# The first block's rotary step: partner dimension read across partitions by VectorE instead of produced by a TensorE product

## The reference, cut to what matters

```
def apply_rope(t, cos, sin):
    tf = t.astype(jnp.float32).reshape(*t.shape[:-1], HEAD_DIM // 2, 2)
    c = cos[None, :, None, :]
    s = sin[None, :, None, :]
    t0, t1 = tf[..., 0], tf[..., 1]
    out = jnp.stack([t0 * c - t1 * s, t0 * s + t1 * c], axis=-1)
    return out.reshape(t.shape).astype(t.dtype)
...
        q = apply_rope(split_heads_norm(q, q_norm[layer], N_HEADS), cos, sin)
        k = apply_rope(split_heads_norm(k, k_norm[layer], N_KV_HEADS), cos, sin)
...
        attn = latent_attention(q, k, v, kc, vc)
```

## Time and profile before

| | |
|---|---|
| median of 3 runs | 2101.53 us |
| profiled execution, its span | 2097.6 us |
| busy: TensorE, weight loads, VectorE, ScalarE | 91%, 74%, 54%, 43% of the span |
| heads of layer 0 (about 51 to 125 us), of layer 1 (about 909 to 957 us) | 74 us, 48 us |
| instructions of the rotation product L923 | 40, two for each of 20 products |

### The profile page before, as it was taken

How to read it: one execution, slowest core, us unless ns; L and a number is a source line. 1 busy time by engine, 2 the same in 40 slices (tenths; PEclk the granted TensorE clock), 3 DMA queues, 4 the chain that set the end, 5 groups by cost and what they waited for, 6 DMA issues and landing times.

```text
span 2097.6 us, 33677 instructions
## 1 busy us (share of the span) xinstructions
PE 1903.2 (91%) x14126; PEld 1550.1 (74%) x14126; DVE 1133.1 (54%) x1862; ACT 892.0 (43%) x1516; POOL 16.9 (1%) x31
## 2 busy tenths in 40 slices
PE   7999989999999999999899999999999667777666
PEld 4877677778777888899699999997898444455444
DVE  3454766676787789557655667789665111110012
ACT  4333444565766667445444555644845000000001
POOL 0000000000000000000000000000000000000000
PEclk9999999999999999999999999999999998998888
DMA  8222014453555555224045555543247999999995
GB/s 313 88 71 80 1 72 143 162 202 104 170 172 180 191 193 177 89 93 161 1 167 196 171 188 185 183 161 121 81 151 304 419 421 419 419 419 420 421 420 233
DMA packets 91121, 428.00 MB, mean 204 GB/s; under 512 B 11089, under 2 KB 12754, under 8 KB 66002
## 3 DMA queue, kind: packets, MB, share of 16 engines
q1 hardware_dynamic: 78866, 382.51, 48.3%
q10 hardware_dynamic: 12096, 43.26, 6.1%
HBM read 424.68 MB, written 1.05 MB: 203 GB/s over the span
## 4 chain that ended last, share of the span: by engine, by line
PE 66%; DMA 19%; DVE 7%; ACT 3%; SPq 2%; issue 2%; DVEq 0%; POOL 0%; ACTq 0%; POOLq 0%
PE bank L463 43%; PE bank L1608 8%; DMA area<-in_w 7%; DMA ring<-in_w 4%; DMA his<-in_w 4%; DMA PPT<-in_w 2%; PE bank L478 2%; PE bank L2453 2%; DMA HH<-in_w 1%; DVE st L1270 1%; PE bank L1198 1%; SPq L2890 1%; PE bank L2497 1%; PE bank L2104 1%; ACT PPT L1215 1%
## 5 line engine op out<-in xcount | busy, mean ns | idle before, releaser
L463 PE MATMUL bank<-HH_r,his_r 128*128 128x256 f32 (+1 forms) x1504 | 505.0, 336 | 3.8 <-DVE ring_r L442 3.7
L463 PE MATMUL bank<-HH_r,ring_r 128*128 128x256 f32 (+1 forms) x1504 | 490.7, 326 | 0.0
L442 DVE TENSOR_TENSOR ring_r<-ring,his_r 128x1024 fp32r<-128x1024 f32 x306 | 373.7, 1223 | 216.2 <-ACT his_r L434 214.9
L463 PE MATMUL bank<-H_r,his_r 128*128 128x256 f32 (+1 forms) x1440 | 471.0, 327 | 0.0
L434 ACT ACTIVATE his_r<-ring 128x1024 fp32r<-128x1024 f32 x306 | 322.5, 1056 | 317.7 <-PE bank L463 234.1
L463 PEld LDWEIGHTS bank<-HH_r,his_r 128*128 128x128 f32 x1504 | 283.7, 189 | 38.0 <-issue 13.4
L463 PEld LDWEIGHTS bank<-HH_r,ring_r 128*128 128x128 f32 x1504 | 283.2, 188 | 27.1
L463 PEld LDWEIGHTS bank<-H_r,his_r 128*128 128x128 f32 x1440 | 270.9, 188 | 28.5 <-issue 2.6
L2469 DVE TENSOR_TENSOR tmp<-tmp,bank 128x128 f32<-128x128 f32 x64 | 18.4, 288 | 386.7 <-ACT tmp L2462 268.4
L2453 PE MATMUL bank<-area,KF 128*32 128x128 f32 x1888 | 88.3, 315 | 41.2 <-DMA area<-in_w 36.7
L463 PE MATMUL bank<-area_r,his_r 128*128 128x256 f32 (+1 forms) x384 | 122.1, 318 | 0.0
(11 more groups left out here) (412 smaller groups left out, 3318.4 us busy)
## 6 DMA issues: line engine op xcount, KB each, us to landing
area<-in_w SPq DMA_DIRECT2D x91, 1024.0 KB, 27.3
ring<-in_w_in SPq DMA_DIRECT2D x102, 512.0 KB, 3.5
ring<-in_w_gate_up SPq DMA_DIRECT2D x88, 512.0 KB, 3.5
ring<-in_w SPq DMA_DIRECT2D x36, 1024.0 KB, 27.1
HH<-in_w SPq DMA_DIRECT2D x26, 1024.0 KB, 26.8
ring<-in_w_down SPq DMA_DIRECT2D x44, 512.0 KB, 3.5
KX<-in_w_mod_rows ACTq DMA_DIRECT2D x28, 512.0 KB, 3.4
VX<-in_w_mod_rows ACTq DMA_DIRECT2D x28, 512.0 KB, 3.5
```

The source lines that it names most:

```text
L442: ve.eng.tensor_tensor(lo_slot(u), stream.slot(u), hi_slot(n).bitcast(F32), ALU.subtract).then_inc(*ve_lo.up(n))
L463: ins = pe.eng.matmul(out, a, b, start=k == 0 and m == 0, stop=end)
```

## The change: what it does

The order of the 128 dimensions of each query and key head of the first block becomes: the 64 even ones, then the 64 odd ones. This is done on the host, in the columns of w_in and in the two norm gains (`halves`). The cosine and sine tables follow that order, the sine negated for the second half. A dimension's partner then lies 64 partitions away. The rotation product and its matrix go; VectorE multiplies, in two operations on 64 partitions each, one half of the head by the sine table of that half and writes the result to the other half of tmp[2]. It then waits for both before it overwrites the head with the cosine product. The constants become two columns narrower.

```diff
-CON = {"ident": 0, "sel": 128, "rope": 130, "cos": 258, "sin": 514, "dftc": 770, ...}
+CON = {"ident": 0, "sel": 128, "cos": 256, "sin": 512, "dftc": 768, ...}
-NCON = 2818
+NCON = 2816
...
-        def pe_rope_step(pe, l, i):
-            out = banks.take((ve_rope, ("sin", l, i)), "rope", l, i)
-            pe.wait_ge(*banks.emptied("rope", l, i))
-            pe.wait_ge(*landed["dft"])
-            pe.wait_ge(*ac_out.at("head", l, i))
-            pe.eng.matmul(out[:, 0:256], cc("rope"), heads(l)[i][3][:, 0:256], start=True, stop=True).then_inc(*pe_rope.up(l, i))
...
             pe_head_sums(pe, l, 0)
-            pe_rope_step(pe, l, 0)
             pe_values_projected(pe, l)
             pe_head_sums(pe, l, 1)
-            pe_rope_step(pe, l, 1)
...
                 if i > 2:
                     pe_head_sums(pe, l, i - 1)
-                    pe_rope_step(pe, l, i - 1)
...
             pe_head_sums(pe, l, 9)
-            pe_rope_step(pe, l, 9)
...
         def ve_rope_step(ve, l, i):
             x = heads(l)[i][3][:, 0:256]
             ve.wait_ge(*ve_rope.last())
-            ve.wait_ge(*pe_rope.at(l, i))
-            ve.eng.tensor_tensor(tmp[2][:, 0:256], banks.ap("rope", l, i)[:, 0:256], cc("sin", 0, 256),
-                                 ALU.mult).then_inc(*ve_rope.up("sin", l, i))
+            ve.wait_ge(*landed["dft"])
+            ve.wait_ge(*ac_out.at("head", l, i))
+            for to, of in ((slice(0, 64), slice(64, P)), (slice(64, P), slice(0, 64))):
+                ve.eng.tensor_tensor(tmp[2][to, 0:256], x[of, :], cc("sin", 0, 256)[of, :],
+                                     ALU.mult).then_inc(*ve_rope.up("sin", l, i, to.start))
+            ve.wait_ge(*ve_rope.last())
             ve.eng.tensor_tensor(x, x, cc("cos", 0, 256), ALU.mult).then_inc(*ve_rope.up("cos", l, i))
             ve.wait_ge(*ve_rope.last())
             ve.eng.tensor_tensor(x, x, tmp[2][:, 0:256], ALU.add).then_inc(*ve_rope.up("roped", l, i))
...
+def halves(w):
+
+    a = w.reshape(w.shape[:-1] + (-1, 64, 2))
+    return np.swapaxes(a, -1, -2).reshape(w.shape)
...
-        put(("q_norm", l), cols(I["q_norm"][l]))
-        put(("k_norm", l), cols(I["k_norm"][l]))
+        put(("q_norm", l), cols(halves(I["q_norm"][l])))
+        put(("k_norm", l), cols(halves(I["k_norm"][l])))
...
-        "w_in": tiles(I["w_in"], paired(W_IN_ORDER, 8, (10,))),
+        "w_in": tiles(np.concatenate([halves(I["w_in"][:, :, 0:1280]), I["w_in"][:, :, 1280:]], axis=2), paired(W_IN_ORDER, 8, (10,))),
```

More of the change, by code:

```diff
@@ L72 @@
 NVEC = _vec_layout()
-CON = {"ident": 0, "sel": 128, "rope": 130, "cos": 258, "sin": 514, "dftc": 770, "dfts": 1282, "idfc": 1794, "idfs": 2306}
+CON = {"ident": 0, "sel": 128, "cos": 256, "sin": 512, "dftc": 768, "dfts": 1280, "idfc": 1792, "idfs": 2304}
 NCON0 = 130
-NCON = 2818
+NCON = 2816
 FIL = {"z": 0, "decay": 256}
@@ L84, in shape_constants @@
     con[:, 0:128] = np.eye(P)
-    for i in range(64):
-        con[2 * i + 1, CON["rope"] + 2 * i] = -1.0
-        con[2 * i, CON["rope"] + 2 * i + 1] = 1.0
     late = np.zeros((P, 3, P), np.float32)
@@ L97, in shape_constants @@
     ang = np.concatenate([row[:, None] * inv, col[:, None] * inv], axis=1).astype(np.float32)
-    con[:, CON["cos"]:CON["sin"]] = np.repeat(np.cos(ang.astype(np.float64)), 2, axis=1).T
-    con[:, CON["sin"]:CON["dftc"]] = np.repeat(np.sin(ang.astype(np.float64)), 2, axis=1).T
+    con[:, CON["cos"]:CON["sin"]] = np.tile(np.cos(ang.astype(np.float64)).T, (2, 1))
+    con[:, CON["sin"]:CON["dftc"]] = np.concatenate([np.sin(ang.astype(np.float64)).T, -np.sin(ang.astype(np.float64)).T])
     t = np.arange(256, dtype=np.float64)
```

## The result

| | runs | median | ratio to the kernel before, 95% interval |
|---|---|---|---|
| kernel before | 4 | 2100.97 us | |
| changed kernel | 4 | 2109.57 us | 1.0047 (1.0031 to 1.0063) |

The account below looks back on a forecast made before the run. TensorE's instruction stream was taken as the bound: 18 products x 0.43 = 7.7 us off the 2097.6 us span gives 2089.9, plus 3.9 around it gives 2093.8 us; range 2091.0 to 2098.5.

Parts of the forecast that it names:

- What bounds the stage: In the query/key heads of both layers, TensorE's instruction stream is the bound, with the rotation product standing in it.
- 0.43 us a product, 18 of 20: In both layers' heads, each removed rotation product saves TensorE 0.43 us; 18 of 20 count, 7.7 us in all.
- Index 8 gives nothing: Removing head index 8's product saves nothing in either layer, because the next sums wait for ScalarE's square of the last head.
- VectorE's halves, bounds 0.34 to 0.84, taken 0.45: Each half operation takes 0.45 us start to start; VectorE gets 11.2 us more in all, beside TensorE, costing nothing.
- Two columns fewer ... cost taken as nothing (a rival below): Narrower constants put every SBUF tensor behind them 8 bytes lower, or a multiple of the allocator's step; cost nothing.
- Rival (c): Moved SBUF addresses slow VectorE and ScalarE operations behind the constants: 3.7% cancels the gain, 6% gives 2106.4 us; chance 0.05.
- The shift at 957 us is not the shift at the end: Sign of a wrong prediction: everything behind layer 1's heads, ending at 957 us, should come 7.7 us earlier through the end.

Follow-up runs that it names:

- e11: e4's kernel with each of the two half operations on VectorE made twice: 2098.09 us, ratio 0.9988.
- e4: Changed kernel with 32 unused bytes per partition directly ahead of the weight ring, small tensors left where the change put them: 2093.14 us, ratio 0.9963.
- e12: Kernel before without the rotation product; VectorE multiplies the head itself by the sine table in one operation, rotation not computed: 2094.55 us, ratio 0.9971.
- e1: Changed kernel with two unused columns at the end of the constants, making them 2818 wide again: 2094.63 us, ratio 0.9967.
- e9: Kernel before with its two epsilons moved into another small tensor, so ring and high parts lie where the changed kernel has them: 2121.11 us, ratio 1.0088.
- e8: Kernel before with 32 unused bytes per partition ahead of all tensors: 2100.11 us, ratio 1.0001.

## Why the prediction was wrong, step by step

- **What bounds the stage**: right. The chain in both head stages is TensorE's, and when VectorE is made to be the bound (e11) the time shows it.
- **0.43 us a product, 18 of 20**: right. Period 3.27 us and the 0.11 us slower first matmul (2.94) in e4 and e12; 7.7 us forecast, 6.9, 7.8 and 6.1 us measured in e1, e4 and e12 (from the ratios), each with an interval of 2.4 to 3.0 us either way. It did not all come where it was forecast. In e4 and e12 the heads of layer 0 end 4.2 us earlier than before, but the next 48 matmuls take 12.70 us instead of 11.00, and the 168 matmuls start only 2.5 us earlier, not 3.9.
- **Index 8 gives nothing**: right, in both layers. In layer 0 of the changed kernel the sums start out of a wait at 119.88 and take 1.05 us. But with the product gone TensorE sits idle for 0.48 us between the two groups of one-column sums (up to 119.51 in e4), where it was busy throughout before; the prediction had no term for that. In e4 the granted clock then fell, from about 120.7 us, to 0.50, that is 1.2 GHz, and was back at 1.00 by 125:

```profile
121.00:124.00 3.00, 3.00 (x8) 2.35 (x8) 1.84 (x3) 1.00 (x2) 0.00 (x0) 0.50 0.05 14
```

  These are the 1.7 us of the point above. The clock fell there in three of the eight profiled executions without the product (e4, e11, e12) and in none of the six with it. In e1, with the same 0.48 us, it stayed at 1.00 and the 48 matmuls took 11.11 us, so the idle time alone does not decide it.
- **VectorE's halves, bounds 0.34 to 0.84, taken 0.45**: right. In the changed kernel two halves together take 0.87 us, that is 0.45 from start to start and 0.42 for one. Its timeline in layer 1:

```profile
943.55 1.23 DVE L439 TENSOR_TENSOR ring_r<-ring,his_r 128x1024 fp32r<-128x1024 f32 x1
944.81 0.87 DVE L988 TENSOR_TENSOR tmp<-area,con 64x256 f32<-64x256 f32 x2
945.71 0.42 DVE L991 TENSOR_TENSOR area<-area,con 128x256 f32<-128x256 f32 x1
946.17 0.42 DVE L993 TENSOR_TENSOR area<-area,tmp 128x256 f32<-128x256 f32 x1
946.88 1.23 DVE L439 TENSOR_TENSOR ring_r<-ring,his_r 128x1024 fp32r<-128x1024 f32 x1 [0.29 <-ACT his_r L431]
```

  The halves start at once behind the split and no longer wait for TensorE; the idle time in front of the next split, 0.29 us, is all that VectorE has left in a head. There is no wait between the halves, yet the second starts 0.45 us after the first, and not 0.34 as cos behind sin did. The Trainium skill, "VectorE: DVE Perf Modes", section "Two Vector instructions with no wait between them", has an instruction whose start quadrant differs from the last one's held until the earlier ones have finished; the trace agrees.
- **"Two columns fewer ... cost taken as nothing (a rival below)"**: this is the step that failed. It cost 0.88% of the time when done alone (e9), 18 us where the sum had nothing, more than twice the gain that I had worked out. The forecast holds for the change without it: e1, the changed kernel with its tensors in place, has a median of 2094.63 us against the 2093.8 predicted.
- **Rival (c)** named the cause, the moved addresses, and gave the right sign, with a chance of 0.05. I priced it on the wrong engine. I asked what VectorE and ScalarE, 10% of the chain, would have to lose and found 3.7% for zero gain; the argument against, that their operations with different start addresses differ by 0.02 us, was sound for them: VectorE is busy 1143.9 us in the changed kernel and 1143.7 in e1, ScalarE 892.8 and 892.3. TensorE reads the moved ring too and holds 66% of the chain: about 1,400 us, most of it matmuls that read the ring, and 0.6% of it cancels the gain. I had no row on what a shift does to matmuls, which should have widened the bounds instead of making the term nothing; the range ended at 2098.5.
- **"The shift at 957 us is not the shift at the end"** was named as a sign of being wrong, and it is the one that showed: +0.3 and +11.5 us.

## What to carry to other kernels

An edit that changes the size of any on-chip tensor is two edits: what it says, and a new place for every tensor behind it. Compare stretches of untouched matmuls in both traces before reading anything else, and more than one: the 576 matmuls above would have told of 5.7% where the others agree on 1.9%. If they moved while the clock didn't, pad the tensor back to its old size and time again before judging the idea. Where a kernel is paced by TensorE, the distance between the buffers for weights and activations is worth a sweep of its own, for each shape of matmul, since the best place of one shape was a bad one for the other.

## What the runs showed of the hardware

- TensorE at full clock and busy throughout ran the same fp32r matmuls 1.9% slower, or 1.0% and 3.8% faster, with the distance of the two tensors that they read: 336 matmuls of 256 columns took 38.09 to 40.32 us, 168 of 512 columns 38.11 to 39.23 us, over seven distances modulo 256. At equal distance the figures of different kernels agreed to 0.02 us in these two stretches (six kernels at distance 192). Moving both tensors together by 32 bytes changed nothing.
- Distance isn't all. In the profiled execution of the kernel before, the 576 matmuls from 1166.76 us took 65.53 us, 0.114 us each, at full clock and distance 192; e8, the same program 32 bytes up, took 68.08 us, and e1, e4, e11 and e12 took 67.84 to 68.08. The kernel before has only one profile; what let it run faster there stays open.
- 128 bytes are not the period (0 and 128 differ). Whether 256 bytes are one, no run tests, and which two reads get in each other's way I did not separate: that the weight load of the next matmul meets the columns streaming for this one is an argument, not shown. For ring and high parts apart nothing was tried either.
- The 96 matmuls of the values, which stream the weights and hold the activations, took 10.89 us in layer 0 before, 11.50 after, but also 11.00 in e4, 11.31 in e8 and 11.41 in e1 at the old distance, and in e12 11.01 in layer 0 and 11.41 in layer 1; what sets them apart stays open.
- VectorE reads partitions 64 to 127 and writes 0 to 63 in the 0.42 us of a plain operation with 256 columns; half the partitions save nothing.
